# A two-layer backbone step: 40 tokens' expert rows gathered ahead of the other gathered rows, a first tile chosen in portions, part sums folded from DRAM

## What is computed

```python
def peer(h, w_pq, sub_keys, expert_u, expert_v):
    qh = (t @ w_pq).reshape(T, PEER_HEADS, 2, D_HALF)
    scores = jnp.einsum('thpd,hpkd->thpk', qh, sub_keys)
    s_top, i_top = lax.top_k(scores, PEER_TOPK)
    cand = s_top[:, :, 0, :, None] + s_top[:, :, 1, None, :]
    best, pos = lax.top_k(cand.reshape(T, PEER_HEADS, -1), PEER_TOPK)
    idx = jnp.take_along_axis(cand_idx.reshape(...), pos, axis=-1)
    gate = jax.nn.softmax(best, axis=-1)
    act = jax.nn.gelu(jnp.einsum('td,thkd->thk', tb, expert_u[ib]))
    return jnp.einsum('thk,thkd->td', gb * act, expert_v[ib])
```

## Time and profile before

| What | Value |
|---|---|
| median of 3 runs | 3855.42 us (3853.39 to 3858.77) |
| the profiled execution, its own time | 3875.16 us |
| its span on the core | 3873.4 us |
| TensorE matmul busy | 3671.6 us, 95% of the span |
| VectorE, ScalarE, GpSimd busy | 68%, 16%, 49% |
| DMA moved | 1093.38 MB, mean 282 GB/s |
| granted TensorE clock, mean | 0.983 |

### The profile page before, as it was taken

How to read it: one execution, slowest core, us unless ns; L and a number is a source line. 1 busy time by engine, 2 the same in 40 slices (tenths; PEclk the granted TensorE clock), 3 DMA queues, 4 the chain that set the end, 5 groups by cost and what they waited for, 6 DMA issues and landing times. The chain is left out here.

```text
span 3873.4 us, 45253 instructions
## 1 busy us (share of the span) xinstructions
PE 3671.6 (95%) x15378; PEld 2526.1 (65%) x15378; DVE 2617.9 (68%) x5597; ACT 629.5 (16%) x1542; POOL 1881.6 (49%) x1565
## 2 busy tenths in 40 slices
PE   7999997899999999999989999879999999999998
PEld 3445576667677666666755456776666776676666
DVE  4424598758776676666765256886678666767776
ACT  3212217400000000000021121381000000000000
POOL 0011039636756666666502100693476565766663
PEclk9999999999999999999999999999999999999999
DMA  9710208879999999999950121197899999999997
GB/s 397 299 61 28 98 13 125 189 264 397 408 383 391 395 390 408 408 408 408 383 191 39 42 81 43 34 161 229 320 408 408 360 409 400 399 408 408 408 408 280
DMA packets 488301, 1093.38 MB, mean 282 GB/s; under 512 B 200612, under 2 KB 237572, under 8 KB 487140
## 3 DMA queue, kind: packets, MB, share of 16 engines
q0 software_dynamic: 170496, 620.83, 40.6%
q1 hardware_dynamic: 315716, 461.43, 35.3%
q10 hardware_dynamic: 1952, 9.57, 0.7%
HBM read 1048.74 MB, written 42.89 MB: 282 GB/s over the span
## 5 line engine op out<-in xcount | busy, mean ns | idle before, releaser
L1492 PE MATMUL ps<-big,y_nat 128*128 128x344 f32 x4096 | 1249.1, 458 | 50.0 <-DMA y_nat<-in_peer_ut 40.8
L1492 PEld LDWEIGHTS ps<-big,y_nat 128*128 128x128 f32 x4096 | 768.1, 191 | 454.3 <-issue 93.6
L2089 POOL DMA_INDIRECT big<-in_peer_u,gates_area x592 | 771.2, 1303 | 497.3 <-DVE kn_area L1878 328.6
L2100 POOL DMA_INDIRECT big<-in_peer_v,gates_area x592 | 669.4, 1131 | 442.0 <-DVE big L1896 219.1
L1896 DVE SCALAR_TENSOR_TENSOR big<-big,kn_area 128x1024 f32<-128x1024 f32 x592 | 763.0, 1289 | 6.3 <-DVE big L1896 0.5
L1878 DVE CUSTOM_DVE_ANT_0 big<-big,y_nat 128x1024 f32<-128x1024 f32 x592 | 720.8, 1222 | 2.0 <-issue 0.3
L1608 ACT ACTIVATE gates_area<-ps 128x344 f32<-128x344 f32 x256 | 117.0, 457 | 2115.2 <-PE ps L1492 1900.6
L1505 PEld LDWEIGHTS ps<-gates_area,y_nat 128*128 128x128 f32 x2048 | 375.7, 190 | 61.2 <-issue 61.2
L1505 PEld LDWEIGHTS ps<-gates_area,big 128*128 128x128 f32 x2048 | 375.7, 190 | 61.2 <-issue 61.2
L1505 PE MATMUL ps<-gates_area,y_nat 128*128 128x216 f32 x2048 | 394.7, 346 | 0.0
L1505 PE MATMUL ps<-gates_area,big 128*128 128x216 f32 x2048 | 394.7, 346 | 0.0
(11 more groups left out here) (318 smaller groups left out, 3373.2 us busy)
## 6 DMA issues: line engine op xcount, KB each, us to landing
y_nat<-in_peer_ut SPq DMA_DIRECT2D x256, 512.0 KB
y_nat<-in_peer_v SPq DMA_DIRECT2D x128, 512.0 KB
big<-in_peer_v SPq DMA_DIRECT2D x128, 512.0 KB
big<-in_w_mod SPq DMA_DIRECT2D x24, 2048.0 KB, 14.6
expert_gates<-big SPq DMA_DIRECT2D x8, 4096.0 KB, 24.4
gates_area<-expert_gates SPq DMA_DIRECT2D x128, 140.0 KB
kn_area<-expert_gates SPq DMA_DIRECT2D x128, 140.0 KB
big<-in_w_in SPq DMA_DIRECT2D x8, 2048.0 KB, 14.8
```

The costliest lines, as they stand in the source:

```text
L1492: last = pe.matmul(ps[:, 6 + par, 0:NX], u_s[par][:, k, :], h_t[:, k, X0:ND], start=(k == 0), stop=(k == KD - 1))
L2089: pool.indirect_dma_start(out=u_ring[:, k % USLOTS, :], out_offset=None, in_=io["peer_u"][:, :], in_offset=bass.IndirectOffsetOnAxis(ap=ro ...
L2100: pool.indirect_dma_start(out=v_ring[:, k % VSLOTS, :], out_offset=None, in_=io["peer_v"][:, :], in_offset=bass.IndirectOffsetOnAxis(ap=ro ...
```

## The change

The share and part tokens, whose experts are known before the loop, are gathered first. Round 1 is now the parts, round 2 is G0, round 3 CTX. Gathered operations begin at step 1, 4 per step up to step 17, then 5 (2 in four steps) to step 126. G0's choice is cut into pieces over steps 0 to 14 and uses the scratch that CTX's choice uses; the context's key scores are stored to DRAM before the loop and read back at step 7. CTX's choice moves from steps 8 to 45 to steps 24 to 61. Tile rows of G0 and CTX wait in DRAM and are read back behind the two first rounds, the part rows are put in place before the loop, and both the share and part sums go to DRAM and come back at the end.

```diff
-EARLY = 8
+FIRST_AT, NEXT_AT = 0, 24
-ROUNDS = (0, 1, 1 + PH, 1 + 2 * PH, 1 + 2 * PH + P // PARTS // TOPK)
+BUNITS = P // PARTS // TOPK
+ROUNDS = (0, 1, 1 + BUNITS, 1 + BUNITS + PH, 1 + BUNITS + 2 * PH)
-FIRST_GATHER = EARLY + 2
+STEADY, BY_STEP = 18, 4
 def gathered_done(j):
-    steps = range(FIRST_GATHER, N_KEYS - 1)
-    load = lambda s: 2 if s - EARLY in HEAVY else 5
-    share = (2 * UNITS - 1) * TOPK * sum(load(s) for s in steps if s < j) // sum(load(s) for s in steps)
-    return share + min(TOPK, HIDDEN + max(0, j - 1))
+    begun = HIDDEN + BY_STEP * max(0, min(j, STEADY) - 1)
+    steps = range(STEADY, N_KEYS - 1)
+    load = lambda s: 2 if s - NEXT_AT in HEAVY else 5
+    return begun + (2 * UNITS * TOPK - HIDDEN - BY_STEP * (STEADY - 1)) * sum(load(s) for s in steps if s < j) // sum(load(s) for s in steps)
...
@@ sync engine, before the loop
-                    sp.dma_start(ctx_rows[:, :], y_nat[:, CTX, :]).then_inc(s_qs, 16)
-                    sp.wait_ge(s_qs, 32)
+                    for n in range(NG):
+                        sp.dma_start(late_rows[n], y_nat[:, GATHERED[n], :]).then_inc(s_qs, 16)
+                    sp.wait_ge(s_qs, 16 * (1 + NG))
...
+                    for part in range(PARTS):
+                        sp.dma_start(y_nat[XB * part:XB * (part + 1), G0, :], part_rows[0:XB, :]).then_inc(s_qr, 16)
...
+                    sp.wait_ge(s_sbe, 2 * PH)
+                    sp.dma_start(ctx_scores.rearrange("p (g k) -> p g k", k=P), sc_b[:, 1, :, :]).then_inc(s_qs, 16)
...
@@ tensor engine, behind the loop
-                    pe.wait_ge(s_fm, 2)
+                    pe.wait_ge(s_qr, 16 * (XA + PARTS + 4))
                     for n in range(2):
-                        pe.matmul(ps[:, 6 + n, :], fold[:, :], acc[:, n * 512:(n + 1) * 512], ...)
+                        pe.matmul(ps[:, 6 + n, :], fold[:, :], u_ring[:, 7, n * 512:(n + 1) * 512], ...)
@@ scalar engine, in the loop
+                        if j == FIRST_AT + 7:
+                            act.wait_ge(s_tv, 2 * PH)
+                            act.dma_start(sc_4, ctx_scores.rearrange("p (k n) -> p k n", k=KD)).then_inc(s_csl, 16)
...
-                                if u == 2:
-                                    act.dma_start(share_sums[:, :], y_nat[:, CTX, :]).then_inc(s_qs, 16)
-                                if u == 3:
-                                    act.dma_start(y_nat[:, CTX, :], ctx_rows[:, :]).then_inc(s_qr, 16)
-                                if u == PH:
-                                    for part in range(PARTS):
-                                        act.dma_start(y_nat[XB * part:XB * (part + 1), G0, :], part_rows[0:XB, :]).then_inc(s_qr, 16)
                                 if u == UNITS - 1:
-                                    act.dma_start(u_ring[:, 6, :], share_sums[:, :]).then_inc(s_qr, 16)
+                                    for n in range(2):
+                                        act.dma_start(u_ring[:, 6 + n, :], part_sums[n]).then_inc(s_qr, 16)
+                            for n in range(2):
+                                if (kind, u, k) == ("dot", ROUNDS[n + 1] + 1, 6):
+                                    act.wait_ge(s_fm, n + 1)
+                                    act.dma_start(part_sums[n], y_nat[:, UNIT[ROUNDS[n]][1], :]).then_inc(s_qs, 16)
+                                if (kind, u, k) == ("dot", ROUNDS[n + 1] + 1, 13):
+                                    act.dma_start(y_nat[:, UNIT[ROUNDS[n]][1], :], late_rows[n]).then_inc(s_qr, 16)
@@ vector engine
+                    def choose_first(s):
+                        if s < PH - 2:
+                            first_half(s + 2, top_4, index_4, src_4(s + 2), dst_4)
+                            second_half(s + 2, top_4, index_4, dst_4)
+                        if s in (6, 7, 8, 9):
+                            for h in (2 * s - 12, 2 * s - 11):
+                                best_pairs(h, PH + h + 1, G0, cand_4, cut2_4, pos_4)
+                                lane.settle()
+                        if s == 10:
+                            shift(G0, CTX, gate_x4)
...
+                        if s in (11, 12, 13, 14):
+                            resolve_keys(s - 11, G0)
+                        if s == 14:
+                            expert_rows(G0, flat_4)
...
+                    for j in range(N_KEYS):
                         weigh(j, j % 2, j // 2, j - 1 if j >= 2 else None)
+                        choose_first(j - FIRST_AT)
                         gather(j)
+                        choose_next(j - NEXT_AT)
+                    gathered_sums(3)
...
@@ gpsimd
-                    for h in range(PH):
-                        pool.wait_ge(s_tv, PH + h + 1)
-                        pairs(h, top_3, cand_3)
-                    for n in range(USLOTS, rows_before(1, 0)):
-                        u_row(n)
-                    pool.wait_ge(s_rk, 2)
-                    for n in range(VSLOTS):
-                        pool.wait_ge(s_h, EARLY - 1 + n // 4)
-                        v_row(n)
+                    pool.wait_ge(s_sbe, 2 * PH + 1)
+                    pool.wait_ge(s_f, GROUPS)
...
+                        if kind == "dot" and n + USLOTS < rows_before(UNITS, 0):
+                            for i in (2, 3):
+                                if n + USLOTS == rows_before(ROUNDS[i], 0):
+                                    pool.wait_ge(s_rk, i)
                             u_row(n + USLOTS)
+                        if kind == "dot" and u == 0 and (n + 1) % (XA // VSLOTS) == 0:
+                            v_row(n // (XA // VSLOTS))
                         if kind == "add" and 0 <= n and n + VSLOTS < rows_before(UNITS, 0):
                             v_row(n + VSLOTS)
```

More of the change, by code:

```diff
@@ L1522, in _ @@
                     products(1, 16 * (N_KEYS // 2), N_KEYS, last_step=True)
-                    pe.wait_ge(s_fm, 2)
+                    pe.wait_ge(s_qr, 16 * (XA + PARTS + 4))
                     for n in range(2):
-                        pe.matmul(ps[:, 6 + n, :], fold[:, :], acc[:, n * 512:(n + 1) * 512], start=True, stop=False, skip_group_check=True)
-                    pe.wait_ge(s_qr, 16 * (XA + 1 + PARTS + 1))
+                        pe.matmul(ps[:, 6 + n, :], fold[:, :], u_ring[:, 7, n * 512:(n + 1) * 512], start=True, stop=False, skip_group_check=True)
                     for n in range(2):
@@ L1884, in gathered_weights @@
                         i, tile, h = UNIT[u]
-                        gates = (a_gate, exp_gate[:, G0, :], exp_gate[:, CTX, :], part_gate[:, 0, :])[i]
+                        gates = (a_gate, part_gate[:, 0, :], exp_gate[:, G0, :], exp_gate[:, CTX, :])[i]
                         at = slice(0 if u else HIDDEN, TOPK)
@@ L1931, in choose_next @@
                             ranks_of_slots(pos_4, row_4, col_4, rowf_4, colf_4)
[L1932 to L1935 removed]
+                        if s in (30, 32, 34, 36):
+                            resolve_keys(s // 2 - 15, CTX)
                         if s == 37:
@@ L1950, in gathered_sums @@
                         dve.wait_ge(s_ax, i + 1 + rows_before(ROUNDS[i + 1], 0))
-                        if i == 0:
-                            lane.do(dve.tensor_tensor(y_nat[:, CTX, :], acc, gate_b[:, 0, :], ALU.mult), s_fm)
+                        if i < 2:
+                            lane.do(dve.tensor_tensor(y_nat[:, UNIT[ROUNDS[i]][1], :], acc, gate_b[:, 0, :], ALU.mult), s_fm)
                             return
-                        tile = GATHERED[i - 1]
+                        tile = GATHERED[i - 2]
                         lane.do(dve.tensor_tensor(acc, acc, gate_b[:, 1 if tile == CTX else 0, :], ALU.mult))
@@ L1976, in gather @@
                                 if (u, k) == (0, HIDDEN):
-                                    dve.wait_ge(s_qr, 16 * XA)
-                                if (u, k) == (ROUNDS[2], 0):
-                                    dve.wait_ge(s_qr, 16 * (XA + 1))
-                                if (u, k) == (ROUNDS[3], 0):
-                                    dve.wait_ge(s_qr, 16 * (XA + 1 + PARTS))
+                                    dve.wait_ge(s_qr, 16 * (XA + PARTS))
+                                for n in range(2):
+                                    if (u, k) == (ROUNDS[n + 2], 0):
+                                        dve.wait_ge(s_qr, 16 * (XA + PARTS + n + 1))
                                 dot(u, k)
@@ L2081, in rows_at @@
                         at = slice(h * TOPK + k, h * TOPK + k + 1)
-                        return part_idx[:, 0, at] if i == 3 else exp_idx[:, tile, at]
+                        return part_idx[:, 0, at] if i == 1 else exp_idx[:, GATHERED[i - 2], at]
                     def u_row(n):
@@ L2120, in _ @@
                         n = rows_before(u, k)
-                        if kind == "dot" and k == 0:
-                            if u in (3, 4):
-                                for hh in range(4 * (u - 3), 4 * (u - 2)):
```

(17 more changed lines are left out.)

81 lines of the change are left out of this document (28 added, 53 removed).

## The result

The changed kernel took 3833.6 us (median of 4, 3827.4 to 3834.9) against 3856.8 for the kernel before: a ratio of **0.9937** (95% interval 0.992 to 0.9955), 23 us faster. Two later measurements of it, on two chips, gave 0.9940 (0.9924 to 0.9956) and 0.9953 (0.9939 to 0.9966). The forecast was 3804, 51 us saved: the sign was right, the size more than twice too large.

What follows compares the result with a forecast made beforehand. DMA demand at 408 GB/s was taken to set the steady step, just above TensorE's 9.263 us. Losses of 8.5 + 8.5 + 1 = 18 us per layer instead of 42.7 and 43.9 save 51 us: 3804, range 3783 to 3837.

Steps and rivals of the forecast that it cites:

- spreading the gathers: Steady loop steps: fewer gathered tiles per step, 3.81 MB instead of 3.90, cut the loss from 29.0 to 8.5 us per layer.
- rival C: Steady steps: latency of one u stream, not demand, sets the stall; the 29.0 us per layer stay; 3847 us, chance 0.10.
- step 62: One long step per layer, 14.5 us with 5.2 lost, laid to four small part-row DMAs; this loss goes away.
- The burst: Sixteen gathers back to back at steps 8 to 10, 8.5 us lost; moves to the loop's start, again 8.5 per layer.
- The four part DMAs: Part rows sent from ScalarE's queue at step 62; moved before the loop, they save 5.2 us per layer.
- The moves in the loop: 0.5 MB stores and read-backs of sums and rows in the loop, 1.3 us each at 408 GB/s.
- VectorE, GpSimd, SP and the end: Added work and waits on these engines and after the last weigh: cost 0, at most 1 to 2.5 us each.
- Rival A: Loop start: twenty-four tiles in a row cost nothing, 17 us more saved; 3787 us, chance 0.20.
- D: Steps 0 to 17 run at a poor DMA rate, under 317 GB/s; 43 us slower, 3898 us, chance 0.05.
- B: Loop start costs two old bursts, 17 us less saved: 3821 us, up to 3835 with VectorE late; chance 0.17.

Runs made afterwards that it cites:

- experiment 6: The kernel before, with each step's u stream issued ahead of the previous step's v stream: ratio 0.988 to the kernel before.
- experiment 5: The changed kernel, with each step's u stream issued ahead of the previous step's v stream: 3782.1 us, ratio 0.9768 to the kernel before.
- second profile: The kernel before, unchanged, profiled again: span 3856.5 us, ratio 1.0002.
- experiment 3: The kernel before without ScalarE's four DMAs that bring the part rows: 3847.2 us against 3856.9, ratio 0.9974.
- third profile of the changed kernel: The changed kernel, unchanged, profiled again beside the kernel before on one chip: ratio 0.9953 to the kernel before.

## Why the prediction was wrong, point by point

**The step that failed is the term for spreading the gathers: 8.5 us lost per layer in the steady steps.** It measured 25.7 and 21.9. The prediction took the steady loss for bytes against 408 GB/s because 9.56 us of bytes stood beside 9.53 us of step; so it expected the loss to follow the mean demand down. For steps 63 to 127 of the kernel before, demand by itself does give that loss (experiment 6). But a second limit of the same size stood beside it and stayed when the demand fell: in the changed kernel none of the loss is demand (experiment 5). The waits named it, 62 of them for the u stream, and the sum passed it over. Beside the gathers a u stream takes 8.3 us in the median to land and has 8.2 in a step without a stall, and TensorE pays in each step where it takes longer. The load per step sets how often that is: from step 63 to 127, 0.4 to 2 us are lost per layer at 3.15 MB, 8 at 3.48, 13 at 3.81. Whether there would be an edge where demand meets the DMA's limit isn't shown, since the engines were full at a lower rate with halved tiles. This was rival C, at 0.10 and 3847 us: its mechanism was right, but not that the loss would stay whole. The result lies between it and the forecast.

**The demand was there too, behind.** With the window opened, the kernel before loses 20 and 21 us per layer and the changed one 0 and 0.9. In that pair the change is worth 0.988 − 0.9768, some 43 us (46 by the medians), near the 51 that were forecast. That is partly luck: the forecast took the steady steps from 29.0 us per layer to 8.5 and step 62 from 5.2 to nothing; with the window opened the steady steps go from some 20 to nothing, and step 62 loses nothing in either kernel.

**The burst** was priced at 8.5 us before and 8.5 after. Two more profiles of before show 0.7 to 1.5, the changed kernel 2 to 3 in two and 5.8 / 10.5 in one. So the profile's row was high for this kernel, and a term of "no change" was in truth about 1 us per layer against the change, more where SP and ScalarE are late. That the profiled execution lay 0.5% above the median was seen and scaled away. Against the second profile its span is 16.9 us longer: 11.9 in the loops, most of it the burst, and 4.0 between them.

**The four part DMAs** were right: 5.2 us per layer forecast, 10 us measured in all by experiment 3. **The moves in the loop** were priced by bytes, 1.3 us each; the step of the second store lost 1.3 to 4.2 us, but taking it away gave nothing back. **VectorE, GpSimd, SP and the end** at 0 were right: TensorE has no long wait for VectorE's weights in the loop, and from the last gelu to the end it takes 27.9 us before and 27.5 after. **Rival A** (3787) and **D** (3898) didn't happen: from step 1 to 18 the DMA moved 374 and 373 GB/s, above the 317 under which D would decide. Of **B**, there was something at the start: 2 to 3 us per layer in two profiles and up to 10.5 in one, short of two old bursts.

The Trainium skill ("DMA: Bandwidth & Descriptors", Queues, rings and completion order) has each DMA engine take turns between the queues with work. A u stream that lands in 8.3 us while 0.5 MB at 408 GB/s would take 1.3 agrees with sharing. So does the rate by queue: from 2.5 to 7 us after a u stream's issue, SP's queue moves 203 GB/s and the gather queue 201 in the third profile of the changed kernel (medians of 212 steps). The trace doesn't show the turns themselves. The limit of about 358 GB/s per core from its section Bandwidth is not seen: 408 over 300 us, with one core at work.

## What to carry to other kernels

When bytes over rate give the same number as the step, still look at which transfer is waited for and how long it has from issue to need: a step can be both at the DMA's limit and at one stream's window, and only moving the issue tells them apart. In a queue that issues in program order, put the load whose consumer comes first ahead of any wait that isn't its own: one swap of two issues gave 44 us on the kernel before and 66 us by the ratios on the changed one (0.994 to 0.9768; 70 by the medians), the version that beats both. The window to compare with is that of a step without a stall: a median over all steps contains the waits and looks long enough. And take a second profile of the kernel before where a single stall carries a term of the sum.

## What the runs showed of the hardware that was not expected

The DMA ran at 408 GB/s for 300 us with TensorE never waiting: a full DMA cost nothing at 3.81 MB per step once the u stream was issued 13.6 us ahead. At 3.90 MB per step it still cost 20 us per layer. Issued half a microsecond later than usual, the same stream cost 154 us over 254 steps, and the total rate fell to 382 GB/s. With half of the u tiles halved, the engines were full at 371 GB/s. A 0.5 MB store to DRAM in the middle of loads held the rate at 313 GB/s with all engines full, where 380 stood without it; another store of that size did not. The same sixteen gathers in a row cost 8 us in one execution and 1 us in two others: in the first, SP issued a v stream 5.3 us after its release, the u stream 2.8 us behind it, and ScalarE started a gelu 2.9 us late.
